# Prompt attention of a two-layer decoder step: turns of the weights four jobs behind the scores instead of three

## What is computed

```python
# group A, 16 heads x 64: three dilated windows, merged by their denominators (one softmax with a count as bias)
o_a = combine_dilations([dilated_prompt(qa, ka, va, sl_a, w, d) for w, d in A_PATTERNS])
# group B, 16 query heads on 2 key heads: selected blocks and window, each a softmax of its own
o_slc = slc_prompt(qb, ks, vs, idx, sl_b)
o_win = win_prompt(qb, kw, vw, sl_b)
# and for each: s = q k^T - slope * dist;  p = exp(s - max) / sum;  o = p v
```

## Time and profile before

| | us |
|---|---|
| median of three runs | 2526.34 (2525.16 to 2527.83) |
| the profiled execution's own time | 2522.46 |
| its span | 2520.7 |
| this stage, first key turn to last PV | 556 to 804.4 |
| PE busy over the span | 2228.4 (88%) |
| DVE, ACT, POOL busy over the span | 854.5, 717.1, 315.9 |

### The profile page before, as it was taken

One profiled execution on the slowest core, in us unless ns is written; L12 is line 12 of the kernel. 1 busy time (PEld: TensorE's weight loads), 2 busy tenths in 40 slices (PEclk: granted clock), 3 DMA queues, 4 the chain that ended last, 5 costly groups with the idle time before them and its releaser, 6 DMA issues. The chain is left out here.

```text
span 2520.7 us, 34463 instructions
## 1 busy us (share of the span) xinstructions
PE 2228.4 (88%) x13652; PEld 1359.5 (54%) x13652; DVE 854.5 (34%) x2146; ACT 717.1 (28%) x1452; POOL 315.9 (13%) x393
## 2 busy tenths in 40 slices
PE   6999999478897788599679979969999999999798
PEld 3444454364444566488556654436666666566443
DVE  0000000025664344233254422324545444454322
ACT  0001000025664323122135430013444434343300
POOL 0000001103453000144143311000000000000000
PEclk9999999659999899799889989979999999999899
DMA  3232322302112999655334429048988897989710
GB/s 110 75 107 103 80 73 64 58 19 66 51 39 79 415 406 411 243 210 201 119 142 167 156 76 250 0 93 254 290 260 291 248 297 251 300 257 323 251 74 21
DMA packets 207823, 436.87 MB, mean 173 GB/s; under 512 B 59744, under 2 KB 162992, under 8 KB 191024
## 3 DMA queue, kind: packets, MB, share of 16 engines
q1 hardware_dynamic: 199856, 359.29, 43.8%
q0 software_dynamic: 7808, 75.39, 7.9%
HBM read 410.04 MB, written 163.13 MB: 227 GB/s over the span
## 5 line engine op out<-in xcount | busy, mean ns | idle before, releaser
L1901 PE MATMUL rec_bR<-x1T,rec_w 128*128 128x512 f32 x768 | 355.6, 618 | 0.0
L1901 PEld LDWEIGHTS rec_bR<-x1T,rec_w 128*128 128x128 f32 x768 | 147.4, 197 | 172.1 <-issue 171.1
L230 PE MATMUL pab_acc<-xT,pab_w 128*128 128x512 f32 x512 | 224.1, 598 | 10.0 <-DMA pab_w<-in_w_in_ab 10.0
L230 PEld LDWEIGHTS pab_acc<-xT,pab_w 128*128 128x128 f32 x512 | 97.4, 192 | 132.9 <-issue 122.7
L1136 DVE MEMSET kc_p<- 128x32 f32 x1 | 0.1, 85 | 471.2 <-PE cmpp_bP L1082 471.2
L234 PE MATMUL pab_acc<-pab_w,xT 128*128 128x512 f32 (+1 forms) x384 | 155.3, 565 | 0.0
L1239 PE MATMUL cmp_bH<-cmp_xT,cmp_w 128*128 128x256 f32 x512 | 131.5, 382 | 0.0
L548 ACT ACTIVATE ap_sc<-ap_sc,ap_nmax 128x128 f32<-128x128 f32 (+1 forms) x192 | 106.2, 554 | 84.3 <-DVE ap_nmax L578 83.1
L726 PE MATMUL mab_acc<-mab_w,mab_hT 128*128 128x512 f32 x256 | 114.8, 608 | 12.7 <-DMA mab_hT<-scratch_h 12.7
L2276 PE MATMUL out_acc<-out_w,oT 128*128 128x512 f32 x256 | 112.3, 601 | 13.5 <-DMA out_w<-in_w_out_c 13.5
L887 PE MATMUL sa_bT<-ident,sa_ring 128*128 128x128 f32 x640 | 88.8, 298 | 33.2 <-DMA sa_ring<-in_cache_a_k 24.2
(11 more groups left out here) (368 smaller groups left out, 3448.2 us busy)
## 6 DMA issues: line engine op xcount, KB each, us to landing
out<-in_cache_a_k SPq DMA_DIRECT2D x8, 8160.0 KB, 29.7
out<-in_cache_a_v SPq DMA_DIRECT2D x8, 8160.0 KB, 29.6
sa_ring<-in_cache_a_k SPq DMA_DIRECT2D x40, 1024.0 KB, 12.6
sa_ring<-in_cache_a_v SPq DMA_DIRECT2D x40, 1024.0 KB, 20.4
rec_w<-in_w_in_c SPq DMA_DIRECT2D x64, 512.0 KB, 6.8
pab_w<-in_w_in_ab SPq DMA_DIRECT2D x8, 2048.0 KB, 8.1
pab_w<-in_w_in_ab SPq DMA_DIRECT2D x64, 128.0 KB, 3.3
ap_bias<-in_bias_p SPq DMA_DIRECT2D x16, 512.0 KB, 4.2
```

The lines of the kernel that those rows point to most:

```text
L230: last = nc.tensor.matmul(acc[a % 8][:, :], w[u][:, k, j * P:(j + 1) * P], xT[:, k, 0:SEQ], start=(k == 0), stop=(k == KD - 1))
L1901: last = nc.tensor.matmul(bank[:, :], w[h % 2][:, at, k, :], xT[:, k, 0:SEQ], start=(k == 0), stop=(k == KD - 1))
```

## The change

`LAG` goes from 3 to 4, and `RING`, the number of jobs whose scores are kept in `sc`, `nmax`, `den` and `rden`, from 4 to 5. PE's program text is the same, but with LAG = 4 its order over one unit becomes S128, (keys), T2, PV, S256, T4, S384, T6, S512, T8. The copies of turned weights on ACT and DVE move from the end of a step to the front of the next step: in step i both first copy the turn of job i - 5, which PE made in step i - 1. On ACT the copy of the keys then stands ahead of the exponentials of the step, not behind them. On DVE the gate multiplication now stands ahead of the copy that it followed.

```diff
-    LAG, RING = 3, 4
+    LAG, RING = 4, 5
@@ ACT
                 for i in STEPS:
-                    if 0 <= i < NJ:
-                        u, m, cols = job(i)
-                        for h in range(2):
-                            act.wait_ge(s_read, 2 * i + h + 1)
-                            at = sc[i % RING][h][:, 0:cols]
-                            nc.scalar.activation(at, at, ACT.Exp, bias=nmax[:, i % RING, h:h + 1], scale=-1.0,
-                                                 accum_out=den[:, i % RING, h:h + 1]).then_inc(exp_done, 1)
+                    if 0 <= i - 1 - LAG < NJ:
+                        u, m, cols = job(i - 1 - LAG)
+                        act.wait_ge(t_done[0], place[i - 1 - LAG] + 1)
+                        if u >= 2:
+                            act.wait_ge(pv_done, u - 1)
+                        nc.scalar.copy(pT[u % 2][0][:, 0:m + 1, m * P:(m + 1) * P],
+                                       bT[0][:, 0:cols].rearrange("p (j q) -> p j q", q=P)).then_inc(t_read[0], 1)
                     ku = keys_step(i)
...
-                    if 0 <= i - LAG < NJ:
-                        u, m, cols = job(i - LAG)
-                        act.wait_ge(t_done[0], place[i - LAG] + 1)
-                        if u >= 2:
-                            act.wait_ge(pv_done, u - 1)
-                        nc.scalar.copy(pT[u % 2][0][:, 0:m + 1, m * P:(m + 1) * P],
-                                       bT[0][:, 0:cols].rearrange("p (j q) -> p j q", q=P)).then_inc(t_read[0], 1)
+                    if 0 <= i < NJ:
+                        u, m, cols = job(i)
+                        for h in range(2):
+                            act.wait_ge(s_read, 2 * i + h + 1)
+                            at = sc[i % RING][h][:, 0:cols]
+                            nc.scalar.activation(at, at, ACT.Exp, bias=nmax[:, i % RING, h:h + 1], scale=-1.0,
+                                                 accum_out=den[:, i % RING, h:h + 1]).then_inc(exp_done, 1)
@@ DVE
                 for i in STEPS:
+                    if 0 <= i - 1 - LAG < NJ:
+                        u, m, cols = job(i - 1 - LAG)
+                        dve.wait_ge(t_done[1], i - 1 - LAG + 1)
+                        if u >= 2:
+                            dve.wait_ge(pv_done, u - 1)
+                        nc.vector.tensor_copy(pT[u % 2][1][:, 0:m + 1, m * P:(m + 1) * P],
+                                              bT[1][:, 0:cols].rearrange("p (j q) -> p j q", q=P)).then_inc(t_read[1], 1)
                     if 0 <= i < NJ:
...
                         nc.vector.reciprocal(rden[:, (i - 1) % RING, :], den[:, (i - 1) % RING, :]).then_inc(den_ready, 1)
-                    if 0 <= i - LAG < NJ:
-                        u, m, cols = job(i - LAG)
-                        dve.wait_ge(t_done[1], i - LAG + 1)
-                        if u >= 2:
-                            dve.wait_ge(pv_done, u - 1)
-                        nc.vector.tensor_copy(pT[u % 2][1][:, 0:m + 1, m * P:(m + 1) * P],
-                                              bT[1][:, 0:cols].rearrange("p (j q) -> p j q", q=P)).then_inc(t_read[1], 1)
```

## The result

The changed kernel took 2552.9 us (2552.0 to 2554.3, four runs) against 2527.1 in the same comparison: a ratio of **1.0104, interval 1.0086 to 1.0121**, 22 to 31 us slower. Forecast were 2548.1 us, in a range of 2534 to 2559. Sign, place and mechanism were right. The loss is 25.9 us between these medians, for 21.8 in the walk; in the profiled execution the stage alone lost 30.5 us.

The account below looks back on a forecast made before the run. PE was taken to set the pace, waiting for ACT's copies. Units +20.8, end +2.7 and beginning -1.7 gave +21.8 us on 2526.3: 2548.1 us, range 2534 to 2559.

Parts of the forecast that it names:

- the walk: The unit-by-unit reckoning of PE's timeline from trace rows through the stage, giving +21.8 us in all.
- What bounds the stage: PE sets the pace; its 12.6 us of waits before turns are for ACT's copy, none for POOL.
- The W and S units: Units without keys: T2 waits for the 512 job's copy, ahead of PV; 10.15 us, or 11.00 with an S unit's PV.
- The units with keys: Units 2 to 8: the keys' transposes wait for the copy of T8, then T2 for theirs; 11.56 us each.
- The sum: From unit 1's S512 to unit 23's: 239.1 us in place of 218.3, +20.8 us, with no clock cost.
- The end: From the last S512's end to the last PV: 10.5 us in place of 7.8, +2.7 us.
- The beginning: Unit 1's S256 at about 567.5 us in place of 569.28, as unit 2's keys no longer wait for T2: -1.7 us.
- (b): Rival: T2's new wait makes T6's vanish, +11 us, 2537; with the keys' 5 us gain, 2531; chance 0.14.
- The copies in front: ACT's order unchanged in steps without keys; in units with keys the part up to the key copy gets 0.6 us shorter.
- The bank: PE's turns, one PSUM bank for each half: without rotating banks, nothing of the 12.6 us of waiting goes.
- (a): Rival: turns wait for POOL's weights, so the longer lag frees at most 23.6 us: 2503 to 2515; chance 0.07.
- (c): Rival: PE idling lowers its clock in part of the stage, adding about 15 to 21 us: 2563 to 2569; chance 0.05.

Follow-up runs that it names:

- copy between, lag 4: The changed kernel with ACT's copy of half 0 between the two exponentials of the step that made the turn: 2521.3 us, ratio 0.9981.
- the filled kernel: The changed kernel with six and four unread identity transposes in PE's two idle times of seven steps with keys: 2545.1 us, ratio 1.0082.

## Why the prediction was right, and what it missed

- **What bounds the stage** was right: PE waits for ACT's copy, not for POOL. It was argued from the times of single rows against a wait table; adding work to POOL (no change with either lag) and moving the copy by one exponential (T2's wait down by 0.67 us, T6's gone) show it.
- **The W and S units**: forecast 10.15 and 11.00 us, measured 10.16 and 11.0; T2 at 2.90 us after S512 in both; the waits 1.2 to 1.4 and 0.56 us. That PV's place is the cause is shown by moving PV alone.
- **The units with keys**: forecast 11.56 us, and at the upper clock that is what they take (599.50 to 611.01, 11.51, in the changed kernel). But five of them had a PV 1.4 to 1.7 us longer. This is the term that was mis-sized: the clock. The sum had it at nothing within the units, and the prediction gave it 0.05 as a rival; it measured 8.5 us of the stage.
- **Why that term was wrong**: I let it depend on the longest single gap, and 1.37 us at a clock of 1.00 in the A units before (575 to 645 us) seemed to allow anything shorter. The A units of the changed kernel have no longer gap there, but two in a row, 1.09 and 0.77 us with 0.66 of work between, after S128. Four profiled executions have this order of PE (the changed kernel, the same run again, the lag alone, more work for POOL), and 5, 4, 5 and 5 of their seven PVs after these gaps took 3.5 to 4.1 us. Where the pair was 0.62 and 0.77 (copy between, lag 4) one PV of seven took 4.07 us; with 0.77 alone (copies in front, lag 3) none. Filling the gaps removed the long PVs and 9 us. But two gaps in a row are not the whole of it either: in two of the four a W unit's PV took 4.07 us behind a single gap of 1.43, and the same gap in the other W units cost nothing. So idle time of PE is part of the cause, and how much of it in what pattern it takes is not settled by these runs. The Trainium skill, Perfetto Trace Analysis, section Matmul Optimizations, says that TensorE scales its power with its use and that matmuls should run back to back; the 9 us of the filled kernel agree, and I should have given that sentence more weight than 0.05.
- **The sum in the profiled execution**: from unit 1's S512 to unit 23's 247.2 us (573.16 to 820.34), forecast 239.1; the five long PVs are some 7.9 of the 8.1. The end took 12.2 us for 10.5, with an S unit's PV of 4.71 us for 3.16 at a granted clock of 0.69. The beginning gained 2.7 us, not 1.7: unit 1's S256 came about where forecast (568.88, with the stage starting 1.1 us later), and the clock rose sooner. In all that is +30.5 us in the stage (245.2 to 275.7, from the first key turn to the start of the last PV), and the stage ended at 836.0 where the prediction had 826. In the changed kernel run again the end took the 10.5 us of the forecast and the beginning gained 1.8 us, and the stage came out the same, since the units took 248.0 us.
- **How close, and how much of it was luck**: all four kernels with this order have a stage of 278.1 to 278.4 us, +30.5 to +30.9, so the walk was short by some 9 us each time; filling the gaps took 8.5 of them away. The medians of the four differ from the kernel before by 25.9, 29.3, 30.7 and 31.0 us; the result's comparison happened to give the smallest. That its median lies within 5 us of the forecast is in part luck. That it lies in the range is not: even 31.0 us on top of 2526.3 would be 2557.
- **Two slips in the prediction**: with both gains of (b) the time is 2532, not 2531 (21.8 less 11 less 5). And among its signs of being right it had the new wait released by the copy on line 563; the profile names POOL there, and it took experiments to see that it was the copy (line 548 in the changed kernel).
- **The copies in front**: forecast as no change in steps without keys and 0.6 us in those with keys, outweighed by the rest. Alone, they made the kernel about 9 us faster and the stage 5.7, with the A units at 10.0 us for 10.8: 0.6 of that came from the shorter wait for T4, and the wait for T8 is 0.41 where it was 0.75, probably because DVE now does the gate while it waits for T4; that cause was only argued.
- **The bank**: the rule that the prediction cites from the Trainium skill (Perfetto Trace Analysis, section Optimizing Tensor Performance), to rotate through PSUM banks, was not tried, since scores, turns and results take all eight. An earlier copy out of the same bank did what was needed.
- **Of the rivals**, (a), the lag frees the turns, fell. (b), waits only change places, fell. (c) came true in part, at about half of the price that I gave it (9 us for 15 to 21).

## What to carry to other kernels

In a software pipeline written out by hand, a longer lag does not only give slack: it also turns the order of the big pieces against each other. Before choosing one, find the longest chain that returns to the engine that sets the pace, and see which independent work stands in its shadow; here PV covered the 2.2 us from the scores of 512 to their copy, and a lag of 4 moved it out. And when an engine empties a buffer that the pace-setter waits for, put that copy as early as its data allow: between two exponentials rather than behind them was worth 17 to 20 us here.

## What was not expected of the hardware

- TensorE's granted clock fell to its lower level (0.50 from 592.5 to 595.5 us) in an A unit where no gap was longer than 1.1 us, while PE was already busy with the PV behind the gaps, and that PV of 2.38 us took 4.06. It did not fall in every such unit, and ten transposes that nothing reads in each of seven units made the kernel 9 us faster.
- PE's waits before turns were put down to ACT's copy in the kernel before and to POOL in the changed one (32.1 us), though the copy ended those that were followed up in both. POOL's instruction, a semaphore waited for ahead of the same turn, is named here where it had been done for 4.9 us, and making POOL later made the table name it less.
- A POOL that was busy 173 of 276 us (560 to 836) in place of 109 left the stage's time as it was. DVE, which works beside it, was busy 143.2 and 143.1 us of that stretch with the same 591 instructions, so it took no longer for its work.
